# Sparse attention of block 3: values held, weighed probabilities moving, output by features

## What is computed

```python
def one_block(qb):
    ...
    pc = masked_softmax(sc, cmp_end[None, :] <= t[:, None])
    o_c = jnp.einsum('bgrtn,bgnd->bgrtd', pc.astype(vc.dtype), vc)
    ...
    o_s = jnp.einsum('bgrtk,bgtkd->bgrtd', ps.astype(v_sel.dtype), v_sel)
    ...
    o_w = jnp.einsum('bgrtk,bgkd->bgrtd', pw.astype(vwb.dtype), vwb)
    ...
    o = gb[..., 0:1] * o_c + gb[..., 1:2] * o_s + gb[..., 2:3] * o_w
...
o_nsa = nsa_attention(q_nsa, kc, vc, tr(nks), tr(nvs), tr(nkw), tr(nvw), gates)
o_nsa = rms_norm(o_nsa, nsa_norm_g[l])
...
mix = jnp.concatenate([o_nsa.astype(x.dtype), o_hg.astype(x.dtype)], axis=-1) @ w_out[l]
```

## Time and profile before

| | us |
|---|---|
| median of 3 runs | 3020.19 |
| lowest, highest | 3013.92, 3029.64 |
| span of the profiled execution | 3017.7 |
| sparse attention pipeline within it | 2057.86 to 2176.68 |
| norm block behind it | 2176.68 to 2185.97 |

### The profile page before, as it was taken

How to read it: one execution, slowest core, us unless ns; L and a number is a source line. 1 busy time by engine, 2 the same in 40 slices (tenths; PEclk the granted TensorE clock), 3 DMA queues, 4 the chain that set the end, 5 groups by cost and what they waited for, 6 DMA issues and landing times. The chain is left out here.

```text
span 3017.7 us, 38696 instructions
## 1 busy us (share of the span) xinstructions
PE 2912.1 (97%) x15016; PEld 2132.7 (71%) x15016; DVE 1475.9 (49%) x2636; ACT 703.1 (23%) x1710; POOL 179.3 (6%) x229
## 2 busy tenths in 40 slices
PE   8999999999999999999999999999999998999998
PEld 7677857888868768888788887877787663333333
DVE  6654325334443587586543354426665253434345
ACT  2421113220010383481101001105541231111111
POOL 1000000000000120160100001010000010000000
PEclk9999999999999999999999999998899998999999
DMA  5121121222212112201222222222021238999995
GB/s 180 56 99 69 56 91 56 93 98 96 84 58 86 56 30 84 84 13 59 74 94 84 84 106 90 84 80 92 2 72 66 74 128 365 404 422 425 421 423 236
DMA packets 130649, 397.84 MB, mean 132 GB/s; under 512 B 7891, under 2 KB 36964, under 8 KB 109890
## 3 DMA queue, kind: packets, MB, share of 16 engines
q1 hardware_dynamic: 124778, 382.66, 33.1%
q0 software_dynamic: 3728, 6.76, 0.8%
q10 hardware_dynamic: 1992, 6.33, 0.6%
HBM read 395.93 MB, written 4.20 MB: 133 GB/s over the span
## 5 line engine op out<-in xcount | busy, mean ns | idle before, releaser
L782 PE MATMUL bank<-arena 128*128 128x256 f32 x5488 | 1195.0, 380 | 15.3 <-ACT spare L954 3.4
L782 PEld LDWEIGHTS bank<-arena 128*128 128x128 f32 x5488 | 1045.7, 191 | 162.1 <-issue 12.4
L1122 PE MATMUL bank<-arena 128*128 128x256 f32 x1876 | 410.3, 382 | 6.9 <-PEq L132 2.7
L1122 PEld LDWEIGHTS bank<-arena 128*128 128x128 f32 x1876 | 358.9, 192 | 56.5 <-issue 8.6
L846 DVE TENSOR_TENSOR arena<-arena 128x1024 f32<-128x1024 f32 x49 | 60.0, 1226 | 177.8 <-PE bank L782 166.4
L4495 DVE TENSOR_TENSOR arena<-arena,bank 128x512 f32<-128x512 f32 x120 | 82.6, 688 | 126.0 <-PE bank L4379 123.2
L1247 PE MATMUL bank<-arena 128*128 128x512 f32 x304 | 132.1, 593 | 0.0
L1150 DVE TENSOR_TENSOR arena<-arena 128x1024 f32<-128x1024 f32 (+1 forms) x68 | 82.1, 1208 | 101.9 <-PE bank L1122 86.8
L4379 PE MATMUL bank<-arena 128*128 128x512 f32 x256 | 120.9, 605 | 0.0
L4351 PE MATMUL bank<-arena 128*32 128x512 f32 x1016 | 114.3, 594 | 2.9 <-DMA arena<-in_moe_w_up_dram 2.8
L4344 PE MATMUL bank<-arena 128*64 128x512 f32 x256 | 113.3, 596 | 0.0
(11 more groups left out here) (626 smaller groups left out, 3470.2 us busy)
## 6 DMA issues: line engine op xcount, KB each, us to landing
arena<-in_moe_w_up_dram SPq DMA_DIRECT2D x64, 1024.0 KB, 15.9
arena<-in_moe_w_down_dram SPq DMA_DIRECT2D x32, 2048.0 KB, 19.8
arena<-in_moe_w_gate_dram SPq DMA_DIRECT2D x63, 1024.0 KB, 13.7
arena<-in_w_in_dram SPq DMA_DIRECT2D x29, 2048.0 KB, 7.8
arena<-in_w_ff_dram SPq DMA_DIRECT2D x16, 2048.0 KB, 7.8
arena<-in_w_out_dram SPq DMA_DIRECT2D x8, 2048.0 KB, 8.1
arena<-in_w_gate_dram SPq DMA_DIRECT2D x11, 1024.0 KB, 5.3
arena<-in_w_up_dram SPq DMA_DIRECT2D x11, 1024.0 KB, 7.9
```

Of the source, the lines that this page charges most:

```text
L782: last = pe.matmul(bank[:, m, :], lhsT, rhs, start=fresh and m == 0 and k == 0, stop=k == 3, skip_group_check=True)
L1122: last = pe.matmul(bank[:, m, :], x[:, k, m * P:(m + 1) * P], w[:, k, :], start=opening and m == 0 and k == 0, stop=k == w.shape[1] - 1, s ...
```

## The change

The units of a pair of heads are taken branch by branch, and of a branch the four query tiles in a row. GpSimd multiplies the probabilities of a unit by gate / row sum before they are turned; the reciprocal and the gate product run for every unit. Transposes come one step later (unit t-3), and there are three buffers of probabilities. The product with the values waits until two neighbouring query tiles are turned, holds the values (64 columns of weights) and moves the probabilities of both tiles, 256 columns; the first head's output goes to partitions 0 to 63 of the bank, the second's to 64 to 127, so that the three branches add up in PSUM and the output stands by features. VectorE copies it with the gain once per pair of heads, ScalarE squares it, GpSimd adds the squares of the four pairs. The norm block behind the attention is gone: the sum over features is a product of ones with the squares at the start of `gated_recurrence`, root and reciprocal are taken there, and GpSimd multiplies `mixT` by the result inside the recurrence's own norm block. The turns of the memory move to the end of the attention, the clearing of `blocks` to the start of the recurrence.

```diff
-    units = [(j, i, b) for j in range(NH // 2) for i in range(NT) for b in (1, 2, 0)]
+    units = [(j, i, b) for j in range(NH // 2) for b in (1, 2, 0) for i in range(NT)]
     N = len(units)
+    BATCHES = N // (NH // 2) // 2
     width = lambda i, b: (i + 1) * P if b else NCMP
-    tiles = lambda i, b: [(k, P) for k in range(0, (i + 1) * P, P)] if b else [(0, NCMP)]
-    negated = [[c.region(10, (2 * s + a) * 512, S) for a in range(2)] for s in range(2)]
-    probs = [[c.region(10, 2048 + (2 * s + a) * 512, S) for a in range(2)] for s in range(2)]
-    turned = [[c.region(11, (2 * s + a) * 512, S) for a in range(2)] for s in range(2)]
+    tiles = lambda i, b: [(k, P) for k in range(i + 1)] if b else [(0, NCMP)]
+    negated = [[c.region(9, 2048 + (2 * s + a) * 512, S) for a in range(2)] for s in range(2)]
+    probs = [c.region(10, 2048, 2, S), c.region(10, 3072, 2, S), c.region(1, 960, 2, S)]
+    turned = [[c.region(slot, 1024 * a, NT, 2 * P) for a in range(2)] for slot in (6, 11)]
...
+        if u >= 4:
+            eng.wait_ge(mixed.sem, mixed.at(u // 2 - 1))
+        return copy_to_view(eng, turned[u // 2 % 2][a][0:m, 0:n, i % 2 * P:(i % 2 + 1) * P],
+                            c.banks[4 + a][0:m, 0:n * P].rearrange("p (k t) -> p k t", k=n))
...
-                u = t - 2
+                u = t - 3
                 if 0 <= u < N:
                     j, i, b = units[u]
+                    pe.wait_ge(scaled.sem, scaled.at(u + 1))
                     for a in range(2):
-                        pe.wait_ge(exps.sem, exps.at(2 * u + a + 1))
                         if u:
                             copied = (copied_a, copied_v)[a]
                             pe.wait_ge(copied.sem, copied.at(u))
                         for k, m in tiles(i, b):
-                            last = pe.transpose(c.banks[4 + a][0:m, k:k + P], probs[u % 2][a][:, k:k + m], c.ident[:, :])
+                            last = pe.transpose(c.banks[4 + a][0:m, k * P:(k + 1) * P],
+                                                probs[u % 3][:, a, k * P:k * P + m], c.ident[:, :])
                         last.then_inc(flipped.sem, flipped.up())
-                u = t - 3
-                if u >= 0:
+                u = t - 4
+                if u >= 0 and u % 2:
                     j, i, b = units[u]
-                    g = u // 3
                     pe.wait_ge(copied_a.sem, copied_a.at(u + 1))
                     pe.wait_ge(copied_v.sem, copied_v.at(u + 1))
-                    if u % 3 == 0 and g >= 2:
-                        pe.wait_ge(finished.sem, finished.at(g - 1))
-                    bank = c.banks[6 + g % 2]
-                    for a in range(2):
-                        at = (3 * a + b) * NHD
-                        cols = slice((j // 2) * NHD, (j // 2 + 1) * NHD)
-                        for n, (k, m) in enumerate(tiles(i, b)):
-                            value = values[b][:, k // P, cols] if b else values[0][0:m, j // 2, :]
-                            last = pe.matmul(bank[:, at:at + NHD], turned[u % 2][a][0:m, k:k + P], value,
-                                             start=u % 3 == 0 and a == 0 and n == 0, stop=n == len(tiles(i, b)) - 1,
+                    if u % (2 * BATCHES) == 1 and j >= 2:
+                        pe.wait_ge(finished.sem, finished.at(j - 1))
+                        pe.wait_ge(squared.sem, squared.at(j - 1))
+                    bank = c.banks[6 + j % 2]
+                    group = slice((j // 2) * NHD, (j // 2 + 1) * NHD)
+                    for k, m in tiles(i, b):
+                        late = P if b and k == i else 0
+                        for a in range(2):
+                            value = values[b][:, k, group] if b else values[0][0:m, j // 2, :]
+                            last = pe.matmul(bank[a * NHD:(a + 1) * NHD, (i - 1) * P + late:(i + 1) * P], value,
+                                             turned[u // 2 % 2][a][0:m, k, late:2 * P],
+                                             start=u % (2 * BATCHES) == 1 and k == 0, stop=k == len(tiles(i, b)) - 1,
                                              skip_group_check=True)
-                    last.then_inc(added.sem, added.up())
+                    last.then_inc(mixed.sem, mixed.up())
+            pe.wait_ge(lowest.sem, lowest.at(2 * N))
+            memory.turns(pe)
...
-                u = t - 2
+                u = t - 1
+                if 0 <= u < N:
+                    dve.wait_ge(exps.sem, exps.at(2 * u + 2))
+                    dve.reciprocal(pair_of(factor, u), pair_of(total, u)).then_inc(inverted.sem, inverted.up())
+                u = t - 3
                 if 0 <= u < N:
                     copy_turned(dve, u, 1).then_inc(copied_v.sem, copied_v.up())
-                u = t - 4
-                if u >= 0 and u % 3 == 2:
+                u = t - 1
+                if 0 <= u < N:
                     j, i, b = units[u]
...
+                    dve.wait_ge(inverted.sem, inverted.at(u + 1))
+                    dve.tensor_tensor(pair_of(factor, u), pair_of(factor, u), gates[:, i, 6 * j + b:6 * j + b + 4:3],
+                                      ALU.mult).then_inc(weighted.sem, weighted.up())
+                u = t - 5
+                if u >= 0 and u % (2 * BATCHES) == 2 * BATCHES - 1:
+                    j = units[u][0]
+                    dve.wait_ge(mixed.sem, mixed.at(BATCHES * (j + 1)))
+                    dve.tensor_scalar(oT[:, j, :], c.banks[6 + j % 2][:, :], gain[:, j:j + 1], None,
+                                      ALU.mult).then_inc(finished.sem, finished.up())
+            memory.copy_turns(dve, 1, mixed.sem, mixed.at(N // 2))
+            memory.copy_turns(dve, 3, mixed.sem, mixed.at(N // 2))
...
-                        if t >= 2:
-                            act.wait_ge(flipped.sem, flipped.at(2 * (t - 2) + a + 1))
-                        if t >= 12:
-                            act.wait_ge(scaled.sem, scaled.at(t // 3 - 3))
-                        act.activation(probs[t % 2][a][:, 0:n], negated[t % 2][a][:, 0:n], ACT.Exp, bias=least_of(t, a),
+                        if t >= 3:
+                            act.wait_ge(flipped.sem, flipped.at(2 * (t - 3) + 2))
+                        act.activation(probs[t % 3][:, a, 0:n], negated[t % 2][a][:, 0:n], ACT.Exp, bias=least_of(t, a),
                                        scale=-1.0, accum_out=total_of(t, a)).then_inc(exps.sem, exps.up())
+                u = t - 5
+                if u >= 0 and u % (2 * BATCHES) == 2 * BATCHES - 1:
+                    j = units[u][0]
+                    act.wait_ge(finished.sem, finished.at(j + 1))
+                    if j >= 2:
+                        act.wait_ge(added.sem, added.at(j - 1))
+                    act.activation(squares[0 if j == 0 else 1 + (j - 1) % 2], c.banks[6 + j % 2][:, :],
+                                   ACT.Square).then_inc(squared.sem, squared.up())
+            memory.copy_turns(act, 0, mixed.sem, mixed.at(N // 2))
+            memory.copy_turns(act, 2, mixed.sem, mixed.at(N // 2))
...
+        @block.gpsimd
+        def _(pool):
+            pool.memset(eps, EPS3)
+            for t in range(N):
+                j, i, b = units[t]
+                n = width(i, b)
+                pool.wait_ge(weighted.sem, weighted.at(t + 1))
+                pool.tensor_tensor(probs[t % 3][:, :, 0:n], probs[t % 3][:, :, 0:n],
+                                   pair_of(factor, t).unsqueeze(2).to_broadcast([P, 2, n]),
+                                   ALU.mult).then_inc(scaled.sem, scaled.up())
+                if t % (2 * BATCHES) == 8 and j >= 2:
+                    add_square(pool, j - 1)
+            add_square(pool, NH // 2 - 1)
...
-    out = c.region(9, 2048, NT, 512)
-    branch_attention(c, qT, (kcmp, kS, kW), (vcmp, vS, vW), (hide, causal), gates, out)
-    group_rms_to_features(c, out, 1, EPS3, c.region(11, 2048, NT, 512), mixT[:, 0:4, :], c.col["nsa_norm_g_3"],
-                          aside=memory.turns, copies=memory.copy_turns, meanwhile=gated.clear_blocks)
+    squares = [c.region(11, 2912, S), c.region(11, 3424, S), c.region(1, 0, S)]
+    branch_attention(c, qT, (kcmp, kS, kW), (vcmp, vS, vW), (hide, causal), gates, mixT[:, 0:4, :],
+                     c.col["nsa_norm_g_3"], squares, memory, c.small[:, 113:114])
...
+            pool.memset(blocks, 0.0).then_inc(cleared.sem, cleared.up())
...
             near_products(near[0], hk, hq)
+            pe.matmul(near[5][:, :], c.ones[:, :], squares, start=True, stop=True).then_inc(square_sums.sem,
+                                                                                           square_sums.up())
             for v, span in enumerate(spans):
+                if v == 4:
+                    pe.wait_ge(rooted.sem, rooted.at(1))
...
+            dve.wait_ge(rooted.sem, rooted.at(1))
+            dve.reciprocal(inverse, inverse).then_inc(inverted.sem, inverted.up())
...
+                if v == 1:
```

(12 more changed lines are left out.)

81 lines of the change are left out of this document (36 added, 45 removed).

## The result

| | before | after |
|---|---|---|
| median | 3018.19 us (3013.92 to 3029.64, 4 runs) | 2987.49 us (2986.87 to 2994.72, 4 runs) |
| span of the profiled execution | 3017.7 | 2985.1 |
| ratio of the times | | 0.9898, interval 0.9879 to 0.9917 |

The account below looks back on a forecast made before the run. TensorE was taken to bound the attention. Attention -10.5, norm block -9.3 and product with ones +1.2 gave -18.6 us from the 3017.7 span, 2999.1; with 2.5 for the median, 3001.6 us, range 2988 to 3019.

Parts of the forecast that it names:

- The bound: Sparse attention before the change: TensorE bounds it, with 23.5 of 26.1 us per pair of heads accounted for.
- Value products: Attention, probabilities times values: 6.4 us per pair of heads in place of 11.0, with two heads running beside each other.
- The j: One pair of heads (12 units) in the attention: 22.7 us against 26.1, summing the busiest engine over 12 steps.
- PE alone: Attention, lower bound from TensorE's own work per pair of heads: 6.9 + 5.6 + 6.4 = 18.9 us.
- The clock: Attention: half clock cost 7.4 us before and would cost 10 after, with 0 and 28 as far ends.
- The clock stays up: Rival, attention: longer moving streams and fewer loads avoid the 10 us clock loss; 2992 us, chance 0.20.
- Lockstep: Rival, attention: added waits cost what the products save, a pair of heads stays at 26.1 us; 3012 us, chance 0.20.
- No overlap: Rival, value products: the heads' products with different moving data do not overlap; 3019 us, chance 0.06.
- The spread of the half clock: Rival, attention: runs of four compressed units leave PE at 1.2 GHz, 36 us per pair of heads; 3045 us, chance 0.09.
- The norm block: Block behind the attention (squares, roots, normed rows, 16 turns, barrier) goes: 9.3 us less.
- The product with ones: Start of the recurrence, on PE between the first near products: 0.86 to 1.7 us long, delaying by 1.2 us.
- The four multiplies: Recurrence's norm block: near 1.3 us each on an idle GpSimd, under PE's key products, at no cost.

Follow-up runs that it names:

- the denser kernel: Kernel before with the score products of the 256-key units of branches 1 and 2 issued twice into the same bank; 3012.28 us, ratio 0.9978.
- the order mixed: Kernel after with units of a pair of heads run by pairs of query tiles, two of each branch in turn, not four; 2990.2 us, ratio 0.9897.
- the heads are apart: Kernel after with the loop over heads outside the loop over key tiles in the value products, so heads no longer alternate; 2995.94 us, ratio 0.9913.

## Why the prediction was right and wrong, step by step

**The bound: right.** PE bounded the stage before, and bounds it after (20.84 of 21.78 us a j). That the attention lost more than twice the forecast has two sources, the clock (10 us) and the j (3.7 us): together 13.7, which is all of the 108.3 forecast against 94.6.

**Value products: right.** Forecast 6.4 us a j in place of 11.0. Start to start the blocks take 2 x (1.67 + 0.81) + 2 x 0.58 = 6.1. In the kernel before they take 11.6 in the j at full clock, so they save 5.5; transposes give back 0.7, scores 0.3 and idle time 0.2, and 4.3 us a j are left.

**The j: 22.7 forecast, 21.8 measured.** The walk took the busiest engine of every step and added the steps up. The heaviest step was right (3.10 for 3.0), but most light ones were too long: in the j from 2098.92 on, the 12 steps take 0.76, 1.54, 1.19, 2.00, 1.16, 2.85, 1.86, 3.10, 0.92, 2.00, 1.65 and 2.75 us. Where VectorE or ScalarE is the longer one in a step, PE has often caught up a step later, so a sum of maxima by steps lies above the truth. That is 3.7 us over four j. The other end failed as well: PE alone was put at 18.9, and the run without the scaling shows 20.7. Most of that is the transposes, 7.2 us a j for 5.6: the price of 0.116 each was read from a run of eight, and a short block costs more by the piece (two in 0.33 to 0.37 us). Scores take 7.5 for 6.9. The kernel before showed it: 2.6 of the 26.1 us were left open there.

**The clock: the step that failed.** The forecast put 10 us of half clock into the changed stage, and none of it came. It had 7.4 us of loss before and 10 after, and both were wrong; only the second moved the forecast of the time. Before, the loss was what remained of 118.8 after four j of 26.1 and 7 of draining, as if the pipeline filled for nothing lost or gained. But the first j has no transposes and value products of a j before it: in the denser kernel it takes 23.84 against 26.51 us. This 2.7 us of filling (a net value, some low clock is in the 23.84) hid as much of the loss; the run gives 10.0. After, there is no loss inside the stage at all; only its first 4 us are at a low clock (0.60). All nine profiled executions of kernels of the form after, edited or not, keep full clock from 2070 at the latest to the end of the attention. The prediction argued for the drops by short PE work ahead of them (the run of small units in the earlier trace rows), and the change puts four small units in a row. That was the wrong feature to carry over: the clock stayed up with four in a row and with two. The same row has 3.28 us busy of 4.00, and the missing 0.72 is the wait for ScalarE, which the prediction didn't price. The longest idle within a j is 0.54 us in the kernel after. That isn't a rule either: of three such waits of 0.72 us only two had a fall behind them, and with the order mixed PE once waits 0.68 us, near the stage's end, at full clock throughout. The denser kernel shows that a few more products are enough to keep the clock in the kernel before. Whether the kernel after keeps it by its value products moving 256 columns where 64 moved, by its shorter waits, or by something else, no run shows; the cause stays open.

With these numbers the attention adds up: four j -17.2, clock -10.0, filling +2.3 (the kernel after saves only 0.4 us in its first j), drain +0.7 (7.9 against 7.2), together the measured -24.2. Filling and drain of the kernel before are read from the denser one, so this is a split of the difference, and no second measurement of it.

**The rivals.** "The clock stays up" came true; its time, 2992, still had the j at 22.7. Both misses lie on the same side, 10 us of clock and 3.7 us of j, and the range's low end covered little more than the first alone. Lockstep did not come: GpSimd costs 0.9 us a j. "No overlap" is real as a mechanism (7.3 us when the heads are apart) but not in the kernel as written. The spread of the half clock, 3045, did not happen in any of the runs. The Trainium skill's rule of brief idle times (page "TensorE: Matmul & The Clock Gate", section "A second HAM failure mode: psum-queue depth-cycling") gave the wrong sign for the kernel after, where PE still waits three times in a j, for 0.54, 0.22 and 0.17 us, and the clock is 1.00. The kernel before fits it better: each fall in its attention came behind a wait.

**The norm block, -9.3: right.** Its removal shows in full.

**The product with ones, +1.2 for a measured +0.4 in the recurrence.** It takes 2.08 us at half clock, and the second near product ends later by it. VectorE's first span now starts 3.9 us after the recurrence's first product where it was 2.0, mainly because of the idle 2.26 us marked "issue" ahead of the last 15 near products of the first span; before, such a gap (1.80 us) came after 158 products, behind the first span. Against this stands a better clock: 0.66 over the recurrence's first 10 us where it was 0.56. So the near hit holds two terms that weren't in the forecast, and is in part luck. With the mixed order and with no scaling the 128 products run in one go, the clock over the same 10 us is 0.83 and 1.00, and the recurrence takes 41.3 and 40.7 us. What is the gap's share and what the clock's, and what decides where the gap falls, was not tested.

**The four multiplies, 0 for +2.5: wrong.** They were said to lie on an idle GpSimd under PE's key products. Their own length was right, 5.4 us (4 x 1.3 forecast), but VectorE's row of the same stretch wasn't looked at: its steps go from 0.17, 0.69 and 0.69 to 1.15, 1.27 and 1.63 us, and PE waits 2.3 us for the first rows. The Trainium skill names such contention (page "GPSIMD Engine Reference", section "8. Key points": GpSimd shares its SBUF interfaces with VectorE, and they contend when a VectorE instruction has two SBUF inputs or runs in a mode that uses two ports). The trace agrees for L2529 and L2533, and for the gate product with 243 in place of 178 ns. L2521 has one small input and takes 1.15 us too; whether it runs in such a mode no run here shows. VectorE's reading of a bank was untouched (the 512-column minimum 688 ns beside GpSimd's work, 686 before), which is why the scaling did no harm there.

## What to carry to other kernels

When the granted clock falls inside a stage that PE bounds, price the fall by a kernel that holds the clock, not by what is left over in a sum: here a few redundant products gave back 10.0 us, and the change got about as much on top of its own saving. Read PE's idle time just ahead of each fall as well, not only the share of the window, before blaming a kind of work for it. "Hidden on an idle GpSimd" needs a look at VectorE's rows of the same moment; start such work after VectorE's first piece that others wait for. And put the low ends of separate terms together before naming a range.

## What the runs showed of the hardware

- More matrix work can be faster: redundant products of 3.4 us by the price of the earlier trace rows (eight units with 256 columns), and the kernel 0.22% shorter (0.9978, 0.9968 to 0.9988), with a granted clock of 1.00 in place of 0.50 to 0.88 and PE's longest wait down from 0.72 to 0.28 us.
- The clock stayed at 0.50 for 13 us in which PE's rows show no idle time (from 2151 to 2164 in the kernel before; in its second execution 16.00 busy of 16.00 us at 0.57). The fall itself came 1 to 2 us after an idle of 0.72 us.
- Products of 64 output columns in different halves of the array overlap when they alternate one by one (16 in 1.67 us) and not when eight of one half stand ahead of eight of the other (2.58 us).
- VectorE's small step of 4 columns takes 1.15 us in place of 0.17 beside a running GpSimd instruction, a product of 128x512 with two SBUF inputs 1.63 in place of 0.69; the long times move with the GpSimd work.
- A RECIPROCAL of 128x512 on VectorE takes 3.35 us, where a product of that size takes 0.69. In the kernel after it stands in the recurrence, where GpSimd was idle.
